# Conditioning work moved: GpSimd's tiles start later, column sums and gate rows change places, the last norm goes by halves

## The reference, cut to what matters

```python
cond = jax.nn.silu(c)
for l in range(DEPTH_2):
    mod = (cond @ mod_w[l] + mod_b[l]).reshape(B, N_MOD, D)
    m = [mod[:, j, None, :] for j in range(N_MOD)]
    u = modulate(rms_norm_2(h, norm_w[l, 0]), m[0], m[1])      # n * (1 + scale) + shift
    h = h + 0.5 * m[2] * swiglu_2(u, ffn_w_gate[l, 0], ffn_w_up[l, 0], ffn_w_down[l, 0])
    u = modulate(rms_norm_2(h, norm_w[l, 1]), m[3], m[4])
    y = hybrid_mixer(u, ...)
    h = h + m[5] * y
    u = modulate(rms_norm_2(h, norm_w[l, 2]), m[6], m[7])
    h = h + 0.5 * m[8] * swiglu_2(u, ffn_w_gate[l, 1], ffn_w_up[l, 1], ffn_w_down[l, 1])
return h
```

## Time and profile before

| | |
|---|---|
| runs | 4473.6 us median of 3 (4471.9 to 4473.86) |
| profiled execution | 4471.6 us, span 4469.8 us |
| granted TensorE clock | 0.93 on the mean |
| PE busy | 3945.5 us, 88% |
| DVE busy | 2063.5 us, 46% |
| ACT busy | 1445.6 us, 32% |
| POOL busy | 1140.3 us, 26% |

### The profile page before, as it was taken

One profiled execution on the slowest core, in us unless ns is written; L12 is line 12 of the kernel. 1 busy time (PEld: TensorE's weight loads), 2 busy tenths in 40 slices (PEclk: granted clock), 3 DMA queues, 4 the chain that ended last, 5 costly groups with the idle time before them and its releaser, 6 DMA issues.

```text
span 4469.8 us, 45709 instructions
## 1 busy us (share of the span) xinstructions
PE 3945.5 (88%) x17223; PEld 2993.2 (67%) x17223; DVE 2063.5 (46%) x2217; ACT 1445.6 (32%) x1834; POOL 1140.3 (26%) x574
## 2 busy tenths in 40 slices
PE   4998999999998899998999966878998978685999
PEld 3865778757786677875777744854586856573477
DVE  4643656336563465643655434341355442614154
ACT  3344343234332343435433311120243312212033
POOL 4700848108481084710740000200000000200000
PEclk9999999999998999999999987889999988777999
DMA  4733757437572276743654421013554532011453
GB/s 162 260 96 113 251 186 259 118 117 244 198 252 99 89 247 205 240 141 101 219 191 161 131 66 67 1 66 113 169 178 151 184 85 86 1 57 38 159 176 136
DMA packets 493295, 649.55 MB, mean 145 GB/s; under 512 B 16123, under 2 KB 393490, under 8 KB 493138
## 3 DMA queue, kind: packets, MB, share of 16 engines
q1 hardware_dynamic: 471056, 568.52, 38.7%
q0 software_dynamic: 19584, 75.50, 4.9%
q10 hardware_dynamic: 2498, 3.39, 0.2%
HBM read 646.29 MB, written 1.05 MB: 145 GB/s over the span
## 4 chain that ended last, share of the span: by engine, by line
issue 63%; POOLq 18%; PE 10%; POOL 7%; DVE 2%; ACT 1%; DVEq 0%; ACTq 0%
POOLq L527 6%; POOLq L529 6%; POOLq L531 5%; POOL mod_zone L534 3%; PE bank L1062 2%; POOL modrow L534 1%; PE bank L774 1%; PE bank L776 1%; PE bank L775 1%; PE bank L1165 1%; PE bank L1179 1%; PE bank L1181 1%; POOL modrow L517 1%; POOL mod_zone L517 1%; POOL rstd L499 0%
## 5 line engine op out<-in xcount | busy, mean ns | idle before, releaser
L774 PE MATMUL bank<-wproj_hi,x_lo 128*128 128x512 f32 x2112 | 848.0, 402 | 69.9 <-DVE arena L1839 41.7
L776 PE MATMUL bank<-wproj_hi,x_hi 128*128 128x512 f32 x2112 | 830.6, 393 | 0.0
L775 PE MATMUL bank<-wproj_lo,x_hi 128*128 128x512 f32 x2112 | 830.1, 393 | 0.0
L1748 DVE TENSOR_TENSOR wproj_lo<-wproj,wproj_hi 128x2048 fp32r<-128x2048 f32 x252 | 734.4, 2955 | 154.2 <-ACT wproj_hi L1338 154.2
L767 PE MATMUL bank<-wproj,xT 128*128 128x384 f32 (+2 forms) x1728 | 649.7, 533 | 15.4 <-DMA wproj<-in_w_in 10.9
L767 PEld LDWEIGHTS bank<-wproj,xT 128*128 128x128 f32 x1728 | 326.9, 193 | 311.2 <-issue 186.6
L497 POOL TENSOR_SCALAR rstd<-sumsq 128x1 f32<-128x1 f32 x38 | 8.2, 216 | 2043.7 <-ACT tok L1321 2043.7
L774 PEld LDWEIGHTS bank<-wproj_hi,x_lo 128*128 128x128 f32 x2112 | 401.5, 190 | 159.7 <-DVE arena L1839 45.1
L1338 ACT CAST wproj_hi<-wproj 128x2048 fp32r<-128x2048 f32 x252 | 469.1, 1910 | 8.7 <-DMA wproj<-in_ffn_w_gate_up 6.6
L776 PEld LDWEIGHTS bank<-wproj_hi,x_hi 128*128 128x128 f32 x2112 | 400.9, 190 | 86.8
L775 PEld LDWEIGHTS bank<-wproj_lo,x_hi 128*128 128x128 f32 x2112 | 402.3, 190 | 80.9 <-issue 1.0
(11 more groups left out here) (387 smaller groups left out, 4855.2 us busy)
## 6 DMA issues: line engine op xcount, KB each, us to landing
wproj<-in_ffn_w_gate_up SPq DMA_DIRECT2D x336, 512.0 KB, 5.8
wdown<-in_ffn_w_down SPq DMA_DIRECT2D x132, 1024.0 KB, 5.7
wproj<-in_w_in SPq DMA_DIRECT2D x52, 1024.0 KB, 6.3
wproj<-in_ffn_w_gate SPq DMA_DIRECT2D x84, 512.0 KB, 5.0
wproj<-in_ffn_w_up SPq DMA_DIRECT2D x84, 512.0 KB, 6.0
mod_zone<-in_mod_w POOLq DMA_DIRECT2D x36, 1024.0 KB, 6.5
...
```

The lines of the kernel that those rows point to most:

```text
L774: nc.tensor.matmul(ps, rounded(a_lo), rounded(b), start=first, stop=False, skip_group_check=True)
L775: nc.tensor.matmul(ps, rounded(a), rounded(b_lo), start=False, stop=False, skip_group_check=True)
L776: return nc.tensor.matmul(ps, rounded(a), rounded(b), start=False, stop=final, skip_group_check=True)
L1748: V.tensor_tensor(rounded(wproj_lo[w.odd][:, cols]), src[:, cols], wproj_hi[w.odd][:, cols], ALU.subtract).then_inc(cols_lo, 1)
```

## The change

Five edits go together.

1. `mod_part(i)` waits for `ff_act` to reach 22 i + 4: the activations of the FFN's second step, both halves.
2. At the end of an FFN `turn_act(last)` stands before `mod_sums`.
3. `modulation(l)` is taken apart. Bias, halving and modA go into `mod_columns`, for both layers, on VectorE behind the last `mod_take` in FFN 8. The gate rows of layer l are made inside its first FFN (FFN 9, FFN 11), in steps 1, 2 and 9: VectorE makes one diagonal (`spread_row`) at the head of the step, TensorE multiplies it in two halves into one bank (`mod_row`), one behind the transposes and one behind `gate_up` of half 1, and VectorE copies each half behind an activation (`take_row`).
4. The final norm and the entry of FFN 9 go by halves: half 0's stands between VectorE's two residual additions at the end of FFN 8 (`leave_first_stack`). The entry of half 0 into FFN 11 likewise at the end of FFN 10. TensorE's `turn_x(0, True)` stands behind the last `down` of every second-stack FFN that has one, where it stood before the last twelve instructions.
5. ScalarE issues the small weight DMAs behind `squares()` of the mixer.

```diff
@@ -520,6 +525,7 @@
                 first, last = i * MOD_TILES, (i + 1) * MOD_TILES
+                pool.wait_ge(ff_act, 2 * FF_STEPS * i + 4)
                 for k in range(first, last):
...
@@ -820,23 +828,28 @@
-                def step(st, w, first):
+                def step(st, w, first, row=None):
                     turn_act(st.plus(-1))
+                    if row is not None:
+                        mod_row(row, 0)
                     gate_up(st, w, 1)
+                    if row is not None:
+                        mod_row(row, 1)
                     down(st.plus(-1), first, False)
                 gate_up(Step(n.ffn), Step(n.load), 1)
-                step(Step(n.ffn + 1), Step(n.load + 1), True)
-                step(Step(n.ffn + 2), Step(n.load + 2), False)
+                row = (lambda k: None) if rows is None else (lambda k: 3 * rows + k)
+                step(Step(n.ffn + 1), Step(n.load + 1), True, row(0))
+                step(Step(n.ffn + 2), Step(n.load + 2), False, row(1))
                 with pe.Fori(0, (FF_STEPS - 5) // 2) as j:
                         step(Step(n.ffn + k, j), Step(n.load + k, j), False)
-                step(Step(n.ffn + 9), Step(n.load + 9), False)
+                step(Step(n.ffn + 9), Step(n.load + 9), False, row(2))
                 last = Step(n.ffn + 10)
...
@@ -845,14 +858,16 @@
                 down(last.plus(-1), False, False, (0,))
+                turn_act(last)
                 if not scaled:
                     mod_sums(aux_ps)
-                turn_act(last)
                 down(last, False, True, (0,))
                 down(last.plus(-1), False, False, (1,))
-                if then is not None:
+                if then is not None and not scaled:
                     then()
                 down(last, False, True, (1,))
+                if then is not None and scaled:
+                    then()
...
@@ -1076,16 +1091,14 @@
-            def mod_rows(l):
-                for k in range(3):
-                    pe.wait_ge(diag_ready, 3 * l + k + 1)
-                    for half in range(2):
-                        ps = (proj_ps + down_ps)[2 * k + half]
-                        last = nc.tensor.matmul(ps[:, :], ones[:, 0:P],
-                                                diags[k][:, 4 * half:4 * half + 4].rearrange("p c n -> p (c n)"),
-                                                start=True, stop=True)
-                    last.then_inc(rows_made, 1)
+            def mod_row(row, half):
+                pe.wait_ge(diag_ready, row + 1)
+                pe.wait_ge(rows_taken, 2 * row + half)
+                nc.tensor.matmul(aux_ps[:, :], ones[:, 0:P],
+                                 diag[:, 4 * half:4 * half + 4].rearrange("p c n -> p (c n)"),
+                                 start=True, stop=True).then_inc(rows_made, 1)
...
@@ -1715,18 +1730,19 @@
-            squares()
-            n.hidden += 1
-            for l in range(DEPTH_2):
-                act.wait_ge(hid_ready, 2 * n.hidden)
+            def lora_weights(l):
                 if l == 0:
                     act.dma_start(dst, src).then_inc(small_in, DMA)
-                ffn(True, False, False)
+            for l in range(DEPTH_2):
+                ffn(True, False, False, l == 0)
                 n.hidden += 1
                 squares()
+                lora_weights(l)
                 hybrid(l)
...
@@ -1823,11 +1839,14 @@
-            def ffn(ffn_next, then, row=None):
+            def ffn(ffn_next, then, row=None, layer=None):
                 def step(k, st, w):
+                    spread = {1: 0, 2: 1, 9: 2}.get(k) if layer is not None else None
+                    if spread is not None:
+                        spread_row(layer, spread)
                     for t in range(NT):
...
@@ -1838,6 +1857,10 @@
                                                    gate_sb[:, t, :], ALU.mult, ALU.mult).then_inc(ff_act, 1)
+                        if spread is not None:
+                            take_row(layer, spread, t)
+                    if spread == 2:
+                        layer_scalars(layer)
                     rest_of_rows(st)
...
@@ -1851,6 +1874,10 @@
                     mod_take(aux_ps)
+                    if n.mod == MOD_PARTS:
+                        v.drain()
+                        for l in range(DEPTH_2):
+                            mod_columns(l)
                 n.ffns += 1
...
@@ -2083,36 +2108,39 @@
-            def modulation(l):
-                n.small += SMALL_DMAS * DMA
-                v.drain()
+            def mod_columns(l):
                 V.tensor_tensor(modcol[:, l], modcol[:, l], vec[:, 3 + l, 0:MOD_ROWS], ALU.add)
                     V.tensor_scalar(cols[:, k, 2 * KC:3 * KC], cols[:, k, 2 * KC:3 * KC], 0.5, None, ALU.mult)
-                v.drain()
-                for k in range(3):
-                    V.tensor_tensor(diags[k], ident[:, :].unsqueeze(1).broadcast_to([P, KC, P]),
-                                    cols[:, k, 2 * KC:3 * KC].unsqueeze(2).broadcast_to([P, KC, P]),
-                                    ALU.mult).then_inc(diag_ready, 1)
+                w = vec[:, 1 + l, VEC_2["norm_w"]:VEC_2["norm_w"] + 3 * KC].rearrange("p (a b) -> p a b", a=3)
+                V.scalar_tensor_tensor(modA[:, l], cols[:, :, KC:2 * KC], 1.0, w, ALU.add, ALU.mult)
+            def spread_row(l, k):
+                v.wait_ge(rows_made, 6 * l + 2 * k)
+                V.tensor_tensor(diag, ident[:, :].unsqueeze(1).broadcast_to([P, KC, P]),
+                                modcol[:, l, (3 * k + 2) * KC:(3 * k + 3) * KC].unsqueeze(2)
+                                .broadcast_to([P, KC, P]), ALU.mult).then_inc(diag_ready, 1)
+            def take_row(l, k, half):
+                v.wait_ge(rows_made, 6 * l + 2 * k + half + 1)
+                V.tensor_copy(modrow[:, k, half * 512:(half + 1) * 512], aux_ps[:, :]).then_inc(rows_taken, 1)
+            def layer_scalars(l):
                 mu, ka, sub = VEC_2["mu"], VEC_2["k_a"], VEC_2["subln"]
                                 ALU.mult)
-                v.drain()
-                w = vec[:, 1 + l, VEC_2["norm_w"]:VEC_2["norm_w"] + 3 * KC].rearrange("p (a b) -> p a b", a=3)
-                V.scalar_tensor_tensor(modA[:], cols[:, :, KC:2 * KC], 1.0, w, ALU.add, ALU.mult)
-                for k in range(3):
-                    v.wait_ge(rows_made, 3 * l + k + 1)
-                    for half in range(2):
-                        V.tensor_copy(modrow[:, k, half * 512:(half + 1) * 512], (proj_ps + down_ps)[2 * k + half][:, :])
-                v.drain()
-            def modulated(k):
-                return modA[:, k, :], modcol[:, l, 3 * k * KC:3 * k * KC + KC]
+            def modulated(l, k):
+                return modA[:, l, k, :], modcol[:, l, 3 * k * KC:3 * k * KC + KC]
...
@@ -2426,6 +2454,11 @@
+            def leave_first_stack(t):
+                final_norm(t)
+                enter_ffn(t, modulated(0, 0), True)
             enter_ffn(0, gained(0), False, True)
...
@@ -2443,17 +2476,19 @@
                 else:
-                    ffn(True, nothing)
-            final_norm()
+                    ffn(True, lambda: leave_first_stack(0))
             for l in range(DEPTH_2):
-                modulation(l)
-                enter_ffn(0, modulated(0), True)
-                enter_ffn(1, modulated(0), True)
-                ffn(False, lambda: enter_mix(0, modulated(1), True), row=0)
-                enter_mix(1, modulated(1), True)
-                hybrid(l, lambda: enter_ffn(0, modulated(2), True))
-                enter_ffn(1, modulated(2), True)
-                ffn(l < DEPTH_2 - 1, nothing, row=2)
+                if l == 0:
+                    leave_first_stack(1)
+                else:
+                    enter_ffn(1, modulated(l, 0), True)
+                ffn(False, lambda: enter_mix(0, modulated(l, 1), True), 0, l)
+                enter_mix(1, modulated(l, 1), True)
+                hybrid(l, lambda: enter_ffn(0, modulated(l, 2), True))
+                enter_ffn(1, modulated(l, 2), True)
+                ffn(l < DEPTH_2 - 1, (lambda: enter_ffn(0, modulated(l + 1, 0), True)) if l < DEPTH_2 - 1 else nothing,
+                    2)
 def lam_init(layer):
```

57 lines of the change are left out of this document (31 added, 26 removed).

## The result

Four runs of the changed kernel have a median of 4498.6 us (4488.4 to 4507.4), the kernel before 4473.4 beside them: a ratio of 1.0056, 95% interval 1.0033 to 1.0079. The change made the kernel 25 us slower; forecast were 4478 as the likeliest and 4450 to 4510 as the range. The kernel before spreads over 2 us, the changed one over 19; its profiled run is the fastest of the four. In a second set of five its median was 4498.0 (4494.1 to 4507.5, ratio 1.0061, 1.0047 to 1.0075).

A forecast was written before the change was run, and what follows sets the result against it. TensorE, busy 88% of the span, was taken as the bound, its idle time as the stake. Terms +71.4 - 30 - 11.2 - 21.6 - 4.2 = +4.4 us gave 4478 as a run, range 4450 to 4510.

The forecast's parts named there:

- GpSimd's tiles: FFNs 1 to 8: later tiles save 31.7 us of TensorE wait and 14 of clock, 16 come back: 30 saved.
- 14 of the 16 us of clock: FFNs 1 to 8: the part of the half-clock time behind the eight activation waits that would be saved.
- the meeting: GpSimd's tiles running into VectorE's residue pair in later first-stack steps: 2.0 us per FFN, 16 in all.
- my bound was 46: Upper bound of the saving from later GpSimd tiles in FFNs 1 to 8, if they never meet VectorE's residue pair.
- Column sums: End of each first-stack FFN: sums behind the transposes remove 1.40 us of TensorE idle, 8 times: 11.2 saved.
- The way into the second stack: Into FFNs 9 and 11: half 0 going ahead brings half 1's products 9.5 and 12.1 us earlier: 21.6 saved.
- Into the mixer: FFNs 9 and 11: the last twelve products no longer wait for half 0's transposes, 2.1 us each: 4.2 saved.
- Gate rows: Steps 1, 2, 9 of FFNs 9 and 11: diagonal wait 8.2, products 1.7, clock 2.0 us per row: 71.4 lost.
- (a): Slower rival: GpSimd's tiles still meet the residue pair at full price in each first-stack FFN: 4508 us, chance 0.15.
- (b): Mildly faster rival: GpSimd's tiles never meet the residue pair, saving 46 us: 4462 us, chance 0.17.
- (c): Faster rival: no row wait in FFNs 9 and 11, diagonal ready, rows cost 10 us: 4417 us, chance 0.08.
- (d): Slower rival: first-stack column sums wait for GpSimd's longer tiles, 40 us more: 4518 us, chance 0.07.

The follow-up runs named there:

- e3: Changed kernel with VectorE making each gate row's diagonal one step or more earlier: 4439.7 us.
- e5: e3 with each gate row's second product moved behind the down products: 4424.0 us.
- e9: Changed kernel without half 0 of the tokens going ahead at the two ways into the second stack: 4506.6 us.
- e10: Changed kernel with half 0's transposes again ahead of the last down products in second-stack FFNs: 4505.4 us, ratio 1.0062.
- e2: Changed kernel without GpSimd's wait on ff_act, so its tiles start at once: 4512.9 us.
- e4: Changed kernel with each of GpSimd's nine tiles per FFN waiting for its own step's activations: 4471.9 us.
- e1: The changed kernel run and profiled again, unaltered: 4498.0 us.
- e7: Kernel before plus only GpSimd's wait for the activations of the FFN's second step: 4469.5 us.
- e11: Kernel before with only GpSimd's nine tiles gated one to a step, as in e4: 4444.9 us.
- e6: Changed kernel with both repairs, tiles one to a step (e4) and the gate rows as in e5: 4410.5 us.
- e12: e6 with half 0's transposes ahead of the last down products, as in e10: 4413.5 us.
- e8: Kernel before plus only the column sums behind the transposes at the end of each first-stack FFN: 4462.2 us.

## Why the prediction was right or wrong

The sign and the range of 4450 to 4510 held, and the likeliest value was 20 us too low: the measured 4498.6 lies above the forecast's own 4465 to 4494. Slower by over 0.2% had 0.35 in my chances, behind no clear change with 0.41. Split at FFN 8's last down product, the sum was -41.2 for the first stack and +45.6 for the rest. In the six profiles that share the changed kernel's first stack (its own two, e3, e5, e9, e10) this came out between -8.5 and -30.3, with a median of -19.8; in the four that share its second stack (its own two, e2, e4) the rest came out at +47.3, +41.2, +50.5 and +48.4. The error is in the first stack.

**GpSimd's tiles, -30 forecast; this is the step that failed.** Its waits were nearly right: 10 for the second step (10.3 measured) and 16 for the meeting (18.1), 28.3 in all and so a little over the 10 to 26 that I named. What failed is "14 of the 16 us of clock". In the changed kernel the wait is worth 12 to 15 us, with 13.2 less idle time between e2 and e1; in the kernel before it is worth 3.5, and in e7 TensorE's busy time rose by 6.7 where I had it fall by 14. Even without any meeting at the pair, where my bound was 46, e11 gives 28.4: the idle time saved and no more.

The half clock behind the eight stalls was real, but it did not leave the first stack with them. By the clock records of the two traces TensorE stands at half clock for 170.7 us of the first stack before and for 160.4 in e11. In the first 100 us of the eight FFNs, where the stalls were, this fell from 47.8 to 10.2 us. In the rest of these FFNs it rose from 54.6 to 68.3, and in the mixers from 68.3 to 81.9. Why the low clock turns up there is open, and e11 has one profile. In e6 and e12, where both the stalls and the 1.40 us behind the sums are gone, the first stack's busy time is 2145.5 and 2143.7, 6 to 8 below the kernel before; versions with one and the same first stack differ by more than that (see the spread below).

**Column sums, -11.2.** Right: 10.8 alone, all of it idle time, and no wait for GpSimd, whose nine tiles end 12 to 17 us ahead of the sums.

**The way into the second stack, -21.6.** Near on the spot: half 1's first gate product comes 8.0 to 9.3 us earlier at the first place (forecast 9.5), 10.9 to 12.1 at the second (forecast 12.1). The working gave the halves a share that e9 doesn't show; what is left to explain the gain is that the rows are no longer made there. I had VectorE "free for half 1" as soon as half 0's scale was done, but half 0's copies and its residue come first, so half 1's chain starts where it would without the halves.

**Into the mixer, -4.2.** Wrong: by e10 about +0.4 each. I took away what half 0's transposes had made wait, and not what they had done: behind the last products they and their 2.30 us of wait for the copies lie bare. The size varies with the clock: over all versions with this order the shared wait comes 25.9 to 27.6 us behind the last down product, where it was 24.1, so that the move lies between -1.1 and +0.6.

**Gate rows, +71.4.** Right. The chain is as forecast: six waits, 49.6 us against 49.2. On the spot, from half 1's first gate product to the last down product, FFNs 9 and 11 together took 375.0 us before, or 369.2 without the 2.91 us of wait ahead of the last products in each. They take 435.6 in the first profile and 438.7 in e1, so the rows cost 66.4 and 69.5 us. In e5 the same two stretches take 373.8 and in e6 373.1: the repair takes out 64.9 against e1 and, for e6, 64.1 against e4. That is the 49.7 of wait and 14 to 15 us more, where 12 were forecast for the clock. The row products themselves cost under 5 us net there and not 10.2; the two stretches hold no half clock in e5 and e6, and 6.8 us of it before. In whole runs the repair is worth 74.0 us (e5 against e1) and 61.4 (e6 against e4), where the forecast's waits and clock make 61.2; the two show how little one pair of totals settles. The rest's sum agrees: 41.2 to 50.5 measured, 45.6 forecast.

**The rivals.** (a) gave 4508 with the meeting at full price: the mechanism was not this one, since the wait fell, but the size of the first term was nearer to it than mine. (b), no meeting at all, did not come. (c) was excluded by the new wait and is what e5 builds: 4424, where I had 4417. (d) did not come: the gap in which L534 waited for nothing named, 2.22 before, is 1.23 here. The Trainium skill (same page and section) tells its rule on descriptors of VectorE's two-port modes, and no run here shows that the residues of this kernel run in one; that it had to do with this gap is not shown.

## The spread of the runs

The kernel before lies within 2 to 6 us in every set; each version here spreads over 6 to 20. For e2, with 6 us over five runs, that is no more than the kernel before in the same set (6 over fifteen). The first stack has the same TensorE instructions in the changed kernel, e1, e3, e5, e9 and e10: its idle time is 98.7 to 102.4 us in these six profiles, its busy time 2146.4 to 2164.5. So it is not the waits that differ but the speed at which the same matmuls ran, and a small edit can bring this on (e8 moves four transposes). The clock records say the same. Time at half clock in this stretch is 126.3, 143.4, 146.8, 150.2, 153.6 and 170.7 us in the six, and in that order busy time is 2146.4, 2153.2, 2154.7, 2157.0, 2157.6 and 2164.5.

Some of it arises at the third step's waits, where one and the same wait is followed by a low clock in one run and not in another. Behind the 2.39 us wait in FFN 8 of the first profile, and behind the 2.40 us wait at the same place in e1 (length, TensorE's busy time, clock, DMA share, GB/s):

```profile
2159.13:2165.93 6.80, 6.80 (x32) 1.00 0.57 209
```

```profile
2167.53:2174.33 6.80, 6.79 (x23) 0.75 0.55 205
```

Of the eight such waits one is followed by a low clock in the first profile, two in e1 and in e10, three in e3 and in e5, and six in e9, the slowest of them. But e4 has none of these waits and spreads too. What decides it in a run is open. It means that one profile of such a kernel can't settle an edit of 10 us; the idle time on the spot can.
